# One diffusion-transformer layer on one core: eight places for the conditioning chunks, context attention units between latent ones, norms by halves, and a new head order of the output projection

## What is computed

```
def trunk_layer(x, mod, ...):
    sh1, sc1, g1, sh2, sc2, g2 = jnp.split(mod, 6)       # mod = silu(c) @ w_mod + b_mod
    h = rmsnorm(x, norm1_g) * (1 + sc1) + sh1
    p = einsum('bnd,de->bne', h, w_in)                    # 4608 columns
    ...                                                   # 8 differential heads, 8 grouped-query heads
    o_d = diff_attention(dq1, dq2, dk1, dk2, dv, lam)     # softmax(q1 k1) - lam softmax(q2 k2), times v
    o_d = rmsnorm(o_d, subln_g) * (1.0 - lam_init)        # per head
    o_g = gqa_attention(gq, gk, gv)
    x = x + g1 * einsum('bne,ed->bnd', concat(o_d, o_g), w_out)
    h2 = rmsnorm(x, norm2_g) * (1 + sc2) + sh2
    x = x + g2 * ec_moe(h2, ...)                          # 16 experts, each takes its best tokens
```

## Time and profile before

| | |
|---|---|
| three runs | 2263.48 us median, 2263.16 to 2266.19 |
| the profiled execution | 2266.25 us, of which the span is 2264.1 us |
| TensorE busy | 2118.8 us, 94% of the span |
| VectorE, ScalarE, GpSimd busy | 862.4, 535.2 and 160.2 us |
| conditioning and first block | up to about 149 us |
| rest of the projection | to 623 us |
| attention | 624.7 to 857.5 us |
| output projection and routing | 865.6 to about 1180 us |
| experts and end | to 2264.1 us |

### The profile page before, as it was taken

How to read it: one execution, slowest core, us unless ns; L and a number is a source line. 1 busy time by engine, 2 the same in 40 slices (tenths; PEclk the granted TensorE clock), 3 DMA queues, 4 the chain that set the end, 5 groups by cost and what they waited for, 6 DMA issues and landing times.

```text
span 2264.1 us, 36022 instructions
## 1 busy us (share of the span) xinstructions
PE 2118.8 (94%) x15267; PEld 1167.8 (52%) x15267; DVE 862.4 (38%) x1343; ACT 535.2 (24%) x945; POOL 160.2 (7%) x216
## 2 busy tenths in 40 slices
PE   5899999999999996999949999999999999999992
PEld 2468888778877775878833333333333333233330
DVE  3249878225467764876350111111101111111112
ACT  4432222222267764111111111111101111110112
POOL 1020100000000000221010000000000000000001
PEclk8999999999999987999969999999999999999996
DMA  9876566542300005646459999999999999999996
GB/s 371 319 232 218 210 231 238 212 168 75 121 31 1 1 1 202 215 157 199 187 194 373 397 398 397 403 406 397 408 400 397 398 398 406 402 407 401 398 412 243
DMA packets 126860, 623.82 MB, mean 276 GB/s; under 512 B 12512, under 2 KB 14056, under 8 KB 65952
## 3 DMA queue, kind: packets, MB, share of 16 engines
q1 hardware_dynamic: 103296, 503.89, 56.0%
q0 software_dynamic: 19488, 102.61, 14.4%
q10 hardware_dynamic: 4000, 16.30, 1.9%
HBM read 593.18 MB, written 29.58 MB: 275 GB/s over the span
## 4 chain that ended last, share of the span: by engine, by line
PE 81%; DMA 11%; DVE 4%; ACT 1%; SPq 1%; issue 1%; POOL 0%; DVEq 0%; ACTq 0%; POOLq 0%
PE ps L1088 24%; PE ps L1095 13%; PE ps L641 10%; PE ps L643 10%; PE ps L642 10%; DMA arena<-in_w_expert_up 7%; PE ps L899 3%; PE ps L931 3%; DMA arena<-in_w_mod 3%; PE ps L834 1%; PE ps L913 1%; PE ps L992 1%; SPq L699 1%; PE ps L876 1%; PE ps L1075 1%
## 5 line engine op out<-in xcount | busy, mean ns | idle before, releaser
L1088 PE MATMUL ps<-arena 128*32 128x512 f32 x6144 | 702.1, 594 | 6.9 <-DMA arena<-in_w_expert_up 3.4
L1088 PEld LDWEIGHTS ps<-arena 128*32 128x32 f32 x6144 | 194.4, 110 | 455.3 <-issue 420.8
L1095 PE MATMUL ps<-arena 128*32 128x512 f32 x3072 | 368.0, 593 | 0.0
L641 PE MATMUL ps<-B_w_hi,B_x_hi 128*128 128x512 f32 x720 | 287.6, 399 | 2.5 <-ACT arena L1210 1.2
L642 PE MATMUL ps<-B_w_hi,B_x_lo 128*128 128x512 f32 x720 | 281.6, 391 | 0.0
L643 PE MATMUL ps<-B_w_lo,B_x_hi 128*128 128x512 f32 x720 | 281.5, 391 | 0.0
L1095 PEld LDWEIGHTS ps<-arena 128*32 128x32 f32 x3072 | 98.1, 110 | 223.0 <-issue 223.0
L641 PEld LDWEIGHTS ps<-B_w_hi,B_x_hi 128*128 128x128 f32 x720 | 135.8, 189 | 45.9 <-issue 12.4
L1767 DVE TENSOR_TENSOR B_w_lo<-arena,B_w_hi 128x1024 fp32r<-128x1024 f32 x72 | 87.5, 1221 | 188.8 <-ACT B_w_hi L1250 188.6
L643 PEld LDWEIGHTS ps<-B_w_lo,B_x_hi 128*128 128x128 f32 x720 | 135.7, 188 | 29.3
L642 PEld LDWEIGHTS ps<-B_w_hi,B_x_lo 128*128 128x128 f32 x720 | 135.9, 189 | 26.5
(11 more groups left out here) (221 smaller groups left out, 2025.3 us busy)
## 6 DMA issues: line engine op xcount, KB each, us to landing
arena<-in_w_expert_gate SPq DMA_DIRECT2D x128, 1024.0 KB, 18.5
arena<-in_w_expert_up SPq DMA_DIRECT2D x128, 1024.0 KB, 23.1
arena<-in_w_expert_down SPq DMA_DIRECT2D x128, 1024.0 KB, 22.3
arena<-in_w_mod POOLq DMA_DIRECT2D x48, 1024.0 KB, 5.3
arena<-in_w_in SPq DMA_DIRECT2D x36, 1024.0 KB, 5.2
arena<-in_w_mod SPq DMA_DIRECT2D x64, 512.0 KB, 9.7
arena<-in_w_out SPq DMA_DIRECT2D x16, 1024.0 KB, 6.1
arena<-in_w_mod POOLq DMA_DIRECT2D x64, 256.0 KB, 3.0
```

The costliest lines, as they stand in the source:

```text
L641: eng.matmul(out, x_hi, w_hi, start=start, stop=False)
L1088: mm = pe.matmul(bank(b)[32 * q:32 * q + 32, :], rows[:, 32 * (q % 2):32 * (q % 2) + 32], w_pair[q // 2], start=start, stop=stop, skip_gro ...
L1095: mm = pe.matmul(bank(b)[32 * q:32 * q + 32, :], rows, w_four[q], start=start, stop=stop, skip_group_check=True)
```

## The change

- The ring for conditioning chunks gets eight counters (`PLACES` = 8) and sixteen buffers in the first round; chunk n from 16 on is issued once chunk n - 8 has been used, chunks 8 to 15 once the x tiles or chunks that held their buffers are gone. `LOADS` is written out anew: chunk 7 ahead of `proj` 0, `proj` 1 behind chunk 11, `proj` 2 behind chunk 24, `proj` 3 behind chunk 31.
- After each third latent pair of units a context pair is put into `SEQ`, eight in all; the last eight pairs of the list are latent. Context rows get a buffer of their own.
- The differential norms are made four heads at a time; the turning of groups is planned anew. Two groups are still turned after i = 0 and i = 1; none is turned between attention and the projection.
- `TURNED` is [2, 0, 3, 1]. `HI_AT` places the high parts of heads 0 and 1 in memory that is free early. ScalarE makes the high parts of half chunk 0, heads 0 and 1 and half chunk 1 inside the last two attention steps, VectorE the low parts just behind its last step, and ScalarE copies the late groups between the heads rather than ahead of the next half chunk.
- SyncE issues the reload of x, behind `w_out` chunks 2 and 3; ScalarE issues the load of the gate rows earlier.
- Semaphores of the routing are merged into two.

```
+PLACES = 8
     seq = []
-    for t in range(TL):
-        for j in range(DH):
-            seq += [(t, j), (t, DH + j)]
-    return seq + [(TL, j + DH * i) for j in range(DH) for i in range(2)]
+    for p in range(TL * DH):
+        t, j = p // DH, p % DH
+        seq += [(t, j), (t, DH + j)]
+        if p % 3 == 2 and p // 3 < DH:
+            seq += [(TL, p // 3), (TL, DH + p // 3)]
+    return seq
...
-TURNED = [2, 3, 0, 1]
+TURNED = [2, 0, 3, 1]
+HI_AT = [10, 11, *range(10), *range(12, 16)]
...
+    order = [("mod", n) for n in range(PLACES)] + [("proj", 0)]
+    order += [("mod", n) for n in range(8, 12)] + [("proj", 1)]
+    order += [("mod", n) for n in range(12, 25)] + [("proj", 2)]
+    order += [("mod", n) for n in range(25, N_MODA)]
+    return order + [("proj", c) for c in range(3, 4 * len(ORDER))]
...
             def mod_chunk(n):
-                if RING_A <= n < 12:
-                    sp.wait_ge(mod_landed[s], 32 * (n // RING_A))
-                if n == 7:
-                    after_mod(sp, 0)
-                elif 8 <= n < 12:
+                if 8 <= n < 13:
+                    sp.wait_ge(mod_landed[s], 32)
                     sp.wait_ge(xp_done, transposes_before(("x", n - 8, 3)) + 1)
-                elif 12 <= n < N_MODA:
-                    after_mod(sp, n - RING_A)
+                elif n in (13, 14, 15):
+                    sp.wait_ge(mod_landed[s], 32)
+                    after_mod(sp, n - 9)
+                elif n >= 16:
+                    after_mod(sp, n - PLACES)
...
             out_chunk(3)
+            for t in range(NT):
+                sp.dma_start(x1[:, t, :], x_dram(t)).then_inc(x_in[t], 16)
...
                 ins.then_inc(pt_copied, 1)
-            if is_diff(UNITS - 1):
-                take_diff(UNITS - 1)
-            for i in range(len(OT_AFTER) - 2):
-                take_ot(len(OT_AT) + i, bank(5 + i % 2))
-            act.wait_ge(scored, UNITS)
-            for t in range(NT):
-                act.dma_start(x1[:, t, :], x_dram(t)).then_inc(x_in[t], 16)
-            act.wait_ge(v_out, 32)
+                if u == UNITS - 2:
+                    act.wait_ge(scored, UNITS)
+                    high_out(0)
+                if u == UNITS - 1:
+                    act.wait_ge(v_out, 32)
+                    high_head(0)
+                    high_head(1)
+                    high_out(1)
             act.wait_ge(av_done, UNITS)
+            high_head(2)
+            high_head(3)
+            high_out(2)
+            take_ot(len(OT_AT), bank(5))
+            act.wait_ge(mod_stored, 64)
+            act.dma_start(G1, mod_d[0].partition_broadcast(P)).then_inc(g1_in, 16)
+            for e in range(4, 8):
+                high_head(e)
+            take_ot(len(OT_AT) + 1, bank(6))
+            for e in range(8, HEADS):
+                if e % 4 == 0:
+                    act.wait_ge(ot_taken, len(OT_AT) + e // 4 - 1)
+                high_head(e)
...
-            for h in range(8):
-                if h < HI_D:
-                    high_out(h)
-                for e in (2 * h, 2 * h + 1):
-                    act.activation(oT_hi[e][:, :], oT[:, e, :], ACT.Copy).then_inc(o_hi, 1)
-                if h in (0, 1):
-                    i = len(OT_AFTER) - 2 + h
-                    take_ot(len(OT_AT) + i, bank(5 + i % 2))
...
-            def head_squares(t):
-                after_take(dve, LAST_DIFF[t])
-                od = orow_of(t)[:, 0:DH, :]
+            def head_squares(t, r):
+                after_take(dve, last_of(t, r))
+                hs, v = slice(4 * r, 4 * r + 4), t // TL
+                od = orow_of(t)[:, hs, :]
...
+            low_out(0)
+            low_head(0)
+            low_head(1)
+            take_gqa(UNITS - 1)
+            head_squares(TL - 1, 1)
+            low_out(1)
+            low_head(2)
+            head_norms(TL - 1, 1)
+            low_head(3)
+            low_out(2)
```

More of the change, by code:

```diff
@@ L106, with last_of @@
 assert len(AT) == UNITS and all((j < DH) == (u % 2 == 0) for (_, j), u in AT.items())
-TURNED = [2, 3, 0, 1]
+TURNED = [2, 0, 3, 1]
+HI_AT = [10, 11, *range(10), *range(12, 16)]
 SAME_BEFORE = [sum((j < DH) == (SEQ[u][1] < DH) for _, j in SEQ[:u]) for u in range(UNITS)]
 TAILS = [sum(t < TL and j < DH for t, j in SEQ[:u + 1]) for u in range(UNITS)]
-LAST_DIFF = [max(AT[t, j] for j in range(DH)) for t in range(NT)]
-NORMED = sorted(range(NT), key=lambda t: LAST_DIFF[t])
+NORMED = sorted(((t, r) for t in range(NT) for r in range(2)), key=lambda x: AT[x[0], 4 * x[1] + 3])
+def last_of(t, r):
+    return AT[t, 4 * r + 3]
 def make_turns():
@@ L117, in make_turns @@
     for t in range(NT):
-        want += [(LAST_DIFF[t] + 5, t, r) for r in (0, 1)]
-        want += [(max(AT[t, 4 * r + i] for i in range(4)) + 3, t, r) for r in (2, 3)]
+        want += [(last_of(t, r) + (5 if r < 2 else 3), t, r) for r in range(4)]
     at, after = {}, []
-    for u, t, r in sorted(want, key=lambda x: (x[0] + 9 * (x[1:] in ((TL, 0), (TL, 1))), x)):
+    for u, t, r in sorted(want):
         while u in at:
@@ L132 @@
 OT_LIST = [OT_AT[u] for u in sorted(OT_AT)] + OT_AFTER
-assert len(OT_LIST) == 4 * NT and OT_LIST[-2:] == [(TL, 0), (TL, 1)]
+assert len(OT_LIST) == 4 * NT and OT_AFTER == [(TL - 1, 3), (TL - 1, 1)]
 def group_of(n):
@@ L348, in build @@
         PT = at(W0 + 2560, 2, TOK)
-        orows = [at(W0 + 3840, HEADS, HD), at(H0 + 12 * TOK, HEADS, HD)]
-        assert 12 * TOK + HEADS * HD <= KC * TOK
+        orows = [at(W0 + 3840, HEADS, HD), at(H0 + 12 * TOK, HEADS, HD),
+                 at(W0 + 6912, HEADS, HD)]
+        assert 12 * TOK + HEADS * HD <= KC * TOK and W0 + 6912 + HEADS * HD <= END
         osq = at(W0 + 5888, DH * HD)
@@ L367, in build @@
         assert W0 + 5792 + 8 * P <= E_LAST
-        oT_hi, oT_lo = parts_D["oT_hi"], parts_D["oT_lo"]
+        oT_hi, oT_lo = [parts_D["oT_hi"][i] for i in HI_AT], parts_D["oT_lo"]
         xs = at(H0, D + ROW_PAD)
@@ L438, in build @@
         c_in = sem("c_in")
-        mod_landed = [sem(f"mod_landed{i}") for i in range(RING_A + RING_M)]
+        mod_landed = [sem(f"mod_landed{i}") for i in range(PLACES + RING_M)]
         w_landed = [sem(f"w_landed{i}") for i in range(RING_B)]
@@ L584, in mod_slot @@
             if n < N_MODA:
-                return None, n % RING_A, n // RING_A + 1
+                return None, n % PLACES, n // PLACES + 1
             j = n - N_MODA
-            return M0 + j % RING_M * SLOT, RING_A + j % RING_M, j // RING_M + 1
+            return M0 + j % RING_M * SLOT, PLACES + j % RING_M, j // RING_M + 1
         def quarter_views(n):
[L591 to L595, removed]
+            place = n if n < PLACES else 8 + n % PLACES
+            if place in (4, 5, 13, 14):
+                half = place - 4 if place < 8 else place - 13
+                return at(K0, DH + KVH, TOK + PAST)[:, 4 * half:4 * (half + 1), 0:NB]
+            if place in (6, 15):
+                return at(B0, 4, NB)
+            if place == 7:
+                return at(B0 + SLOT, 4, NB)
+            return at(H0 + place * SLOT if place < 4 else Q0 + (place - 8) * SLOT, 4, NB)
         def after_mod(eng, n):
@@ L1508, in _ @@
             pool.dma_start(new_gv.rearrange("b o t h d -> (b o t) (h d)"), V[:, NT, DH * HD:VW]).then_inc(v_out, 16)
-            for t in range(NT):
-                pool.wait_ge(oms_ready, t + 1)
-                power(ro[:, :], sso[:, :], DH, or_ready)
+            for i, (t, r) in enumerate(NORMED):
+                pool.wait_ge(oms_ready, i + 1)
+                hs = slice(4 * r, 4 * r + 4)
+                power(ro[:, t // TL, hs], sso[:, t // TL, hs], 4, or_ready)
             pool.wait_ge(ot_taken, len(OT_LIST))
@@ L1874, in residual @@
                     dve.tensor_tensor(x1[:, t, cols], x1[:, t, cols], gtmp, ALU.add).then_inc(x1_done, 1)
-            for h in range(8):
-                if h < HI_D:
-                    low_out(h)
-                for e in (2 * h, 2 * h + 1):
-                    dve.wait_ge(o_hi, e + 1)
-                    dve.tensor_tensor(oT_lo[e][:, :], oT[:, e, :], oT_hi[e][:, :].bitcast(F32), ALU.subtract)\
-                        .then_inc(o_lo, 1)
+            for e in range(4, HEADS):
+                low_head(e)
             dve.wait_ge(wr_in, 16)
```

107 lines of the change are left out of this document (47 added, 60 removed).

## The result

The changed kernel takes 2247.16 us (median of four runs, 2245.66 to 2249.36) against 2263.32 us of the kernel before beside it (2262.73 to 2266.19): a ratio of 0.9927, 95% interval 0.9910 to 0.9944. Two more groups of runs gave 0.9898 (0.9885 to 0.9912) and 0.9919 (0.9905 to 0.9933). The forecast was 2243.7 us, -19.8; the three groups have -16.2, -22.5 and -19.1. The profiled execution took 2249.36 us, its span 2247.5 (-16.6).

The account below looks back on a forecast made before the run. TensorE is busy nearly throughout, so its waits and lower clock count: conditioning, attention's end, the way into the output projection. Terms -7.4 + 5.0 - 17.4 = -19.8 take the median 2263.48 to 2243.7 us; range 2232 to 2253.

Parts of the forecast that it names:

- Eight places: Conditioning: transfers no longer pause, chunk 31 at 120.4 instead of 127.83 us; -7.4 us.
- Context pairs: Attention: eight context pairs inserted between latent ones at 3.7 us each, plus 2.5 for turned groups, less 27.1; +5.0 us.
- The bank's chain: Attention: next scores need the same bank, 4.95 us against TensorE's 4.3, adding 0.65 us per inserted pair.
- interleaving doesn't pay by itself: Attention: a context pair in a row cost 3.4 us, and between latent ones it displaces about as much.
- Norms by halves: VectorE in attention: same elements in twice as many instructions, half as long each; taken at nothing.
- Way in: From attention's last values to half chunk 3 of the output projection: 28.5 us against 45.9; -17.4 us.
- half chunk 3 counts as T + 28.5: T is the end of attention's last values; start at T + 25.9, plus 2.6 us longer after the wait.
- T + 23.5: Half chunk 3's start after the last values if the router weights' load lands in 5 us; term then -22.4.
- Everything behind follows: Everything behind half chunk 3, the experts with their transfers too, follows at the same distance.
- Deeper cover: Rival: inserted pair costs 2.9 us, router weights in time; -31, 2232 us (range 2232 to 2238); chance 0.20.
- Little from the conditioning: Rival: splits and `modcopy` hold TensorE at each quarter; conditioning gives -2 to -4, 2247 to 2252 us; chance 0.12.
- The slower ones: Rivals: context steps disturb the latent pipeline, 2250 to 2258 us, chance 0.12; slower, above 6.8 us a pair, chance 0.02.

Follow-up runs that it names:

- second profile: Profile of the changed kernel run once more, unedited: median 2245.99 us, ratio 0.9898 to the kernel before, span 2244.1.
- run 5: Changed kernel with its eight context pairs in a row between latent pairs 24 and 25: 2238.11 us, ratio 0.9881 to the kernel before.
- run 11: Changed kernel with differential norms of latent tiles 0 to 2 and the context tile whole again, only tile 3's by halves: 2248.66 us, ratio 0.9923.
- run 3: Kernel before with the eight places and new order of loads alone, plus four semaphores merged into two: 2258.73 us, ratio 0.9962.
- run 4: Changed kernel with half chunk 3's high and low parts made before heads 8 to 15: 2246.94 us, ratio 0.9901 to the kernel before.
- run 2: Changed kernel with conditioning chunks in four places again, in the old order of loads: 2256.01 us, ratio 0.9939 to the kernel before.

## Why the prediction was right, and where its sizes were off

**Sum.** Forecast -19.8, measured by span -16.6, -20.0 and -20.5. For the second profile the terms are: attention starts -5.4, attention +4.7, way in -21.6, routing -1.0, experts +2.6, end +0.6, together -20.0 (the stages' roundings apart). All of it is against the one profiled execution of the kernel before; the medians have -16.2, -22.5 and -19.1. That the second profile meets the forecast within 0.2 us is in part luck: the way in gave 4.2 more than forecast, and 2.0 less from the conditioning and 2.6 at the experts, a term that I had put at nothing, took most of it back.

**Eight places, -7.4 forecast.** -6.4, -5.4 and -7.0 at the start of attention, -6.8 alone. The turn of the third quarter was forecast at 98.65 and came at 98.51. TensorE's wait was 2.82 and not 1.5, since the clock no longer dropped in the quarter (0.99) and TensorE arrived 1.4 us earlier; that gain went into the wait for ScalarE. Chunk 31 came at 121.30 instead of 120.4: the matmuls behind the wait began at the lower clock. In the second profile that lasted longer (chunk 24 at 105.65 instead of 103.91), hence its -5.4. ScalarE took the `w_in` chunk at 95.97 as forecast (96.0), with 387 GB/s in the window. By an estimate from the bound of about 358 GB/s in the Trainium skill (DMA: Bandwidth & Descriptors, "Where 436 GB/s comes from") it would have been 98.0; the trace of this one core disagrees.

**Context pairs, +5.0 forecast.** 3.7 us a pair forecast, 3.87 measured; +4.7 between executions without a slow first step. The term is nearly right by two misses that cancel: eight pairs at 3.87 are 31.0 and not 29.6, but turning the groups cost less than the 2.5 put on top. Steps with norms and turned groups stretch the latent pairs by 7.4 us in all in the kernel before (seven steps at 6.41 us instead of 6.02, three at 7.58 to 7.60) and by 8.1 in the second profile of the changed kernel, 0.7 more. The bank's chain was priced rightly (0.65 forecast, 0.64 us of wait for the exponentials behind an insertion). The sentence that interleaving doesn't pay by itself held, and more strongly than written: run 5 saves 7.2 us, and part of a row's 27.1 us in the kernel before was lower clock. What the order buys is that latent pairs stand last and that nothing but two groups is left behind attention; for that one row of context pairs ahead of the last tile is enough, as run 5 has it.

**Norms by halves, 0 forecast.** Bounded by run 11: nothing in the median, 2.8 us in favour of the halves in the profile of attention.

**Way in, -17.4 forecast.** -21.6, the term that was mis-sized. The step that failed is "half chunk 3 counts as T + 28.5": the 2.6 us for a low clock behind the wait were paid in no profile of the changed kernel (half chunk 3 lasted 7.9 us as before), and in two profiles of edited kernels at 1.6. (The 2.6 was the loss behind a wait of 6.35 us in the earlier trace rows; behind 3.81 a half chunk lost 2.4 to 2.5 in the kernel before and 1.6 to 2.4 in run 3.) And the router weights landed in 5.9 us instead of 7.6, at 879.2, 0.4 before VectorE had finished the eight low heads, so that half chunk 3 began at T + 24.3, not T + 25.9. I had named the load as what is late last; it nearly tied with the low heads, and run 4, which takes both from in front of half chunk 3's low part, removes the wait. The T + 23.5 for a load in time left out VectorE's 0.75 us for the router weights; with it the sum is T + 24.3, as measured.

No run takes the parts of the new order (heads, places, late copies, latent pairs last) one from another. What the traces show is the sum: in the kernel before 14.0 us of idle ahead of half chunks 0 to 2 (6.35 and twice 3.81) and 7.6 us of lower clock in them, and in the changed kernel neither, but 2.4 us of idle ahead of half chunk 3. That latent pairs need not be spread for it, run 5 shows (T + 24.3 too).

**Everything behind follows.** Nearly. The routing is 0 to 1 us shorter and the experts 1.4 to 2.6 longer than in the single profile of before. Over fourteen profiles with starts from 1147.7 to 1182.6 us the expert stage lasts 1039.7 to 1043.7, with no order by start, so no fixed share is taken back; whether the kernel before was at the short end by chance stays open with one profile of it.

**The rivals.** Deeper cover asked for 2.9 a pair: no. It was right on the way in alone (-22.4 said, -21.6 measured). Little from the conditioning: no, though the splits do stand where it said. The slower ones were far off.

## What to carry to other kernels

Short units didn't pay here as filler between long ones that use the same banks and the same helper engines: measure the price of one inserted pair (here 3.87 us against 2.2 to 2.7 in a row) before spreading them, and let only the tail be of the long kind. When a queue's wait goes, look at what the helper engine does between the landing and the copy that the main engine needs; a step that isn't due belongs behind it. Narrow matmuls that look like pure cost can be the cover of another engine's work, as the late sum was for the residual.

## What the hardware did that I hadn't expected

TensorE's clock fell to the lower level although TensorE was busy throughout: behind sixteen matmuls of one column, four transposes and eight matmuls of sixteen columns (3.0 us together) the next seven ran at 0.63 instead of 0.40 us start to end. It did so in some executions of the same kernel and not in others, at a price of 1.6 us each time (3.1 in run 2, where it lasted 6.8 us); in the profiled executions of the changed kernel two such stretches are 3.2 of the 3.9 us between the longest span and the shortest. The wait of 2.4 us at half chunk 3 was followed by a low stretch in two profiles of nine.
